# A hybrid encoder step on one core: where the moving operands begin, and 35 products behind the last one

## The reference

```
h   = x @ w_in                    # 2048 -> 5124: RG-LRU x and gate, band q,k,v, FoX q,k,v, forget logits
y_A = RG-LRU(conv4(x branch)) * gelu(gate)
y_B = chunk-band attention        # 4 heads of 128
y_C = forgetting attention        # 4 heads of 128
x   = LN1(alpha * x + concat(rms(y_A), rms(y_B), rms(y_C)) @ w_out)
x   = LN2(alpha * x + square(relu(x @ w_up)) @ w_down)      # 2048 -> 8192 -> 2048
```

## Time and profile before

| | |
|---|---|
| median of 3 runs | 2268.21 us |
| profiled execution, from its first to its last instruction | 2264.6 us |
| what lies around it, median less span | 3.6 us |
| PE busy | 2246.3 us (99%), 16556 instructions |
| PE weight loads busy | 2195.6 us |
| DVE busy | 1719.4 us (76%) |
| ACT busy | 1046.0 us (46%) |
| TensorE clock granted | 0.999 of full |
| transfers | 459.60 MB, mean 203 GB/s |

### The profile page before, as it was taken

One profiled execution on the slowest core, in us unless ns is written; L12 is line 12 of the kernel. 1 busy time (PEld: TensorE's weight loads), 2 busy tenths in 40 slices (PEclk: granted clock), 3 DMA queues, 4 the chain that ended last, 5 costly groups with the idle time before them and its releaser, 6 DMA issues.

```text
span 2264.6 us, 38827 instructions
## 1 busy us (share of the span) xinstructions
PE 2246.3 (99%) x16556; PEld 2195.6 (97%) x16556; DVE 1719.4 (76%) x1314; ACT 1046.0 (46%) x1050; POOL 254.7 (11%) x273
## 2 busy tenths in 40 slices
PE   9999999999999999999999999999999999999998
PEld 8999999998889999999999999999999999999997
DVE  5667899885567766767777778778778878878887
ACT  4434566554444456654444444454345235335243
POOL 2010212210111032000000000001112102112101
PEclk9999999999999999999999999999999999999999
DMA  9775766776444487674555455679689789769875
GB/s 289 251 227 163 211 170 188 211 218 221 147 141 131 151 265 227 196 252 150 185 166 183 147 174 169 203 245 241 174 237 244 189 221 260 192 164 292 236 211 178
DMA packets 423343, 459.60 MB, mean 203 GB/s; under 512 B 16376, under 2 KB 398368, under 8 KB 422696
## 3 DMA queue, kind: packets, MB, share of 16 engines
q1 hardware_dynamic: 342608, 358.22, 50.3%
q0 software_dynamic: 36080, 52.64, 13.2%
q10 hardware_dynamic: 44520, 46.80, 6.1%
HBM read 371.12 MB, written 88.05 MB: 203 GB/s over the span
## 4 chain that ended last, share of the span: by engine, by line
PE 86%; DVE 5%; DMA 4%; ACT 2%; issue 1%; SPq 0%; ACTq 0%; DVEq 0%
PE psum L3097 55%; PE psum L2823 17%; PE psum L3066 4%; PE psum L513 4%; DMA raw<-in_w_down 2%; PE psum L3041 1%; DVE w_lo L2153 1%; PE psum L2903 1%; PE psum L2986 1%; PE psum L3002 1%; DVE x_e_lo L2293 1%; DVE w_lo L1706 1%; PE psum L2815 1%; PE psum L2982 0%; DMA kc<-in_cache_band_k 0%
## 5 line engine op out<-in xcount | busy, mean ns | idle before, releaser
L3097 PE MATMUL psum<-x_e_hi,w_hi 128*128 128x288 f32 x1600 | 474.6, 297 | 1.0 <-DVE w_lo L2153 0.8
L3097 PE MATMUL psum<-x_e_hi,w_lo 128*128 128x288 f32 x1600 | 474.2, 296 | 0.0
L3097 PE MATMUL psum<-x_e_lo,w_hi 128*128 128x288 f32 x1600 | 466.8, 292 | 0.0
L3097 PE MATMUL psum<-x_b_hi,w_hi 128*128 128x288 f32 x1536 | 455.4, 296 | 2.6 <-DVE w_lo L2153 1.2
L3097 PE MATMUL psum<-x_b_hi,w_lo 128*128 128x288 f32 x1536 | 455.3, 296 | 0.0
L3097 PE MATMUL psum<-x_b_lo,w_hi 128*128 128x288 f32 x1536 | 447.9, 292 | 0.0
L3097 PEld LDWEIGHTS psum<-x_e_lo,w_hi 128*128 128x128 f32 x1600 | 304.8, 190 | 0.0
L3097 PEld LDWEIGHTS psum<-x_e_hi,w_hi 128*128 128x128 f32 x1600 | 300.7, 188 | 2.7 <-DVE w_lo L2153 2.3
L3097 PEld LDWEIGHTS psum<-x_e_hi,w_lo 128*128 128x128 f32 x1600 | 300.0, 187 | 0.0
L3097 PEld LDWEIGHTS psum<-x_b_lo,w_hi 128*128 128x128 f32 x1536 | 292.8, 191 | 0.1
L3097 PEld LDWEIGHTS psum<-x_b_hi,w_hi 128*128 128x128 f32 x1536 | 288.6, 188 | 3.9 <-issue 2.0
(11 more groups left out here) (434 smaller groups left out, 4859.7 us busy)
## 6 DMA issues: line engine op xcount, KB each, us to landing
raw<-in_w_down SPq DMA_DIRECT2D x61, 1024.0 KB, 7.1
raw<-in_w_up SPq DMA_DIRECT2D x54, 1024.0 KB, 6.5
raw<-in_w_in SPq DMA_DIRECT2D x34, 1024.0 KB, 7.2
a_even<-in_w_down SPq DMA_DIRECT2D x30, 1024.0 KB, 7.2
raw<-in_w_out SPq DMA_DIRECT2D x24, 1024.0 KB, 5.5
a_even<-in_w_up SPq DMA_DIRECT2D x24, 1024.0 KB, 6.8
h_scratch<-c_tile ACTq DMA_DIRECT2D x48, 288.0 KB, 2.3
down_scratch<-c_tile POOLq DMA_DIRECT2D x45, 288.0 KB, 5.0
```

The source lines that it names most:

```text
L3097: mm = pe.matmul(PS[:, bank, 0:HALF], w, x[:, k, :], start=(k + n == 0), stop=(k == UK - 1 and n == 2))
```

## The change

There are two edits. The filler takes 104 bytes in place of 72. The tile behind it begins at 68864 = 538 x 128, and all tiles behind move up by 32 bytes: what began 96 past a multiple of 128 now begins on one. Operands that were at 224 or 96 past a multiple of 256 are now at 0 or 128 past one. Weights, `ident` and `ones` don't move.

Behind the last product PE has 35 more, in fp32r, after a wait for `rows_c` of 20: seven forms, five times each, with `x1_e1_hi` as moving and `w_hi` as stationary operand, into banks 0 to 3. Their results are not read.

```diff
@@ -130,7 +130,7 @@
-        sb("align_64_bytes", [128, 18])
+        sb("align_64_bytes", [128, 26])
@@ -3289,6 +3289,12 @@
+            pe.wait_ge(rows_c, 20)
+            spare_x, spare_w = (t[0][:, :, :].rearrange("p k c -> p (k c)") for t in (F5, WH))
+            for bank, (n, w_cols, x_at, w_at) in enumerate(((288, 96, 0, 0), (288, 64, 0, 0), (288, 128, 0, 16), (288, 128, 0, 8), (256, 128, 0, 0), (320, 128, 0, 0), (384, 128, 0, 0))):
+                for _ in range(5):
+                    pe.matmul(PS[0:w_cols, bank % 4, 0:n], spare_w[:, w_at:w_at + w_cols], spare_x[:, x_at:x_at + n], start=True, stop=True)
```

## The result

The changed kernel is slower. It takes 2274.86 us, the median of 8 runs (2272.8 to 2277.62), beside 2268.66 us for the kernel before (8 runs, 2266.6 to 2274.24). The ratio is 1.0025, with a 95% interval from 1.0015 to 1.0034. The prediction had said 2138 us. The profiled executions have spans of 2271.0 and 2264.6 us: 6.4 us more, about the 6.2 us between the medians.

What follows compares the result with a forecast made beforehand. PE's distance between product starts was taken as the bound. From 2264.6 us, 157 us saved less 27 lost to DVE gave 130 off, 2134.6, plus 3.6 for the median: 2138 us; range 2118 to 2290.

Steps and rivals of the forecast that it cites:

- The first candidate: PE: the weight load as cause of the lost 10 ns; set aside, as it allows a start every 127 ns or less.
- Ten are 133.3 ns, the number of L3066's last units to the tenth.: PE's moving operand: from 96 past, ten blocks of 128 bytes are fetched whole, 13.3 ns each, instead of nine.
- without the tenth block I take 120 ns and the 2.5 ns of the plain products, 122.5: Filler's effect on PE: fp32r products of 288 columns fall from 132.5 to 122.5 ns; 157 us over all lines before losses.
- N: Rival, PE: the loss comes with any fp32r product at one clock a column, so moving operands does nothing; 2268 us, chance 0.18.
- P: Rival, PE: only part is gained, by fetches of 64 bytes (2175 us) or a partial address effect (2221 us); chance 0.15.
- S: Rival, PE: slower, as fetches from the same half of 256 bytes wait; 135.8 ns a product, 2320 us; chance 0.25, mild form included.
- mild form: Milder slower rival, PE: all products cost the dearer half's 133.3 ns; 13 us more, 2281 us; more than half of 0.25.
- a distance that stays over 130 ns: Stated sign on PE that the prediction is wrong: the distance between product starts does not fall below 130 ns.
- The 27 us for DVE at its limit: DVE, late next once PE is faster: takes back 27 us of the gain, 10 at least and 45 at most.
- from 2118 to 2170: Whole kernel: range of the likeliest case, with 10 to 45 us lost and 122.5 to 124.5 ns a product; chance 0.42.
- the 32 bytes do nothing to DVE, ACT and the transfers: DVE, ACT and transfers: their operands move by the same 32 bytes, put at no cost.
- The 35 products were put at nothing: Kernel's end on PE: they take 4.5 us, covered by the last transfer with 2 us to spare, so cost nothing.

Runs made afterwards that it cites:

- e3: The changed kernel with stretches of 24 equal products in place of the 35, moving operand's start varied; 288 columns in fp32r cost 131.7 or 133.3 ns, bf16 122.6.
- e8: The changed kernel with stretches of 24 products in place of the 35, stationary start and width varied too; 32 stationary columns cost 130.4 ns where 128 cost 133.3.
- e9: The changed kernel with fp32r/bf16 pairs, 32-row products and 320 to 480 columns in place of the 35; pairs took 271.1 ns (288 columns) and 460 (512).
- e6: The kernel before with weights moved by 96 bytes and moving operands left in place; 2276.23 us, ratio 1.004, 133.1 ns a product of L3097.
- e7: The change without its 35 products, weights moved by the same 32 bytes as the moving operands; 2266.14 us, ratio 0.999 to before, 132.5 ns in L3097.
- e2: The kernel before, filler of 72 bytes kept, with only the 35 products added; 2269.27 us, ratio 1.0006.

## Why the prediction was wrong, by its steps

*What bounds the kernel, and what a product costs.* Right. PE set the time before and sets it now, 132.5 ns were the distance, 122.5 is what 288 columns cost without the loss (bf16: 122.6), and 10 ns a product were lost. The first candidate was rightly put aside in part: a load of 32 columns gives back 3 of the 10 ns. For the rest the prediction leaned on one product with no load behind it and on L2843, where the distance stays at 133.1 while the stationary operand begins elsewhere with every block. But 133.1 is a mean over 32 products, and a mean over many starts can't show what one of them does. L2843 takes 8.85 us before and 8.84 after: the loss that depends on the address is in it both times.

*"Ten are 133.3 ns, the number of L3066's last units to the tenth."* This step failed, and with it the term of the sum that rests on it, "without the tenth block I take 120 ns and the 2.5 ns of the plain products, 122.5": 10.0 ns less a product were forecast, and 0.6 ns more were measured in L3097. It took 133.3 = 10 x 13.3 for a sign of ten fetched blocks. One number met one formula with a free count in it, and nothing in the trace varied the count. Nine blocks cost 133.4 (e3, L3297) and ten cost 131.7 (L3311). The other support, that plain float32 loses nothing from 96 past a multiple, was true and fitted every account in which four bytes a clock are too many, N's as well: "a new stream that must be filled at double rate". e8 and e9 have that loss from every start, and growing with the columns.

*The second row was there.* The trace showed one line with the same tiles at two prices, 131.8 and 133.3, by a shift of 128 bytes. That was the only effect of an address in the trace, 1.5 ns, and it was noted ("if only 1.5 ns of it"), but the forecast put 10 ns on the address. The change swaps these two cases. By this row alone the time moves by little, in either direction. So it was in L3066, where the two halves changed places.

*The rivals.* N had 2268 us, and P's cause, a smaller unit, is refuted with the forecast's. S in its mild form had 0.8 ns a product, 13 us and 2281; measured are 0.61 ns on L3097, 6.2 us between the medians and 2274.9. The sign was that of S, and in L3097 its words fit, too: all products cost what the dearer ones cost. Its mechanism doesn't fit: by it all products would do so everywhere, but L3066's first half rose from 131.8 to 133.3 while its second fell from 133.3 to 131.7. And what counts is the moving start relative to the stationary one (e6, e7), which none of the four cases had. "All moving operands have the same remainder" was half of the address. The range from 2118 to 2290 us took the measured time in by the shares of N and S, which the forecast spoke against; that is no merit of its sum. By its own sign, a distance that stays over 130 ns, the prediction is wrong.

The Trainium skill (TensorE: Matmul & The Clock Gate, section "Wait — 56ns, not 53.3ns?") has N / 2.4 + 2.5 ns warm, and in its section "Back-to-back issue gap" N / 1.2 cold. bf16 (122.6 by 122.5) and the lower clock (347 by 346.7) agree; fp32r at the higher clock doesn't, by 8 to 16 ns, with the moved start as without. Its lines of 16 bytes (SBUF — State Buffer, section "Door 1: The DMA port swizzle") would have treated before and after alike. Their N was nearer than the forecast, but 1.0025 isn't 1 either, and starts 32 bytes apart, whole lines all, cost 131.7 or 133.3.

*The terms behind the sum.* The 27 us for DVE at its limit were never called on, as PE didn't become faster; whether they were right stays untested. Its case "from 2118 to 2170" was too narrow for its own terms: 124.5 ns a product and 45 us lost are 2187. That the 32 bytes do nothing to DVE, ACT and the transfers held: 2292 ns for `w_lo` of `sigma`, 1917 for `w_hi`, beside the earlier trace rows, and `raw` and `a_even` land after 6.9 and 7.1 us, beside the earlier trace rows. The groups by form after:

```profile
L2153 DVE TENSOR_TENSOR w_lo<-sigma,w_hi 128x2048 fp32r<-128x2048 f32 x56 | 128.4, 2292 | 68.6 <-ACT w_hi L1499 67.2 <-ACT w_hi L1492 1.4
L1499 ACT ACTIVATE w_hi<-sigma 128x2048 fp32r<-128x2048 f32 x55 | 105.4, 1917 | 233.0 <-PE psum L3097 126.1 <-DVE sigma L2139 106.9
```

The 35 products were put at nothing because the last transfer covers them. That held with 1.4 us to spare (2 foreseen), and e2 confirms it. They take 5.4 us in place of 4.5, or of the 5.0 that the price "at 133 ns" had; 0.5 us of it lies between the first start and the second. Their groups of five gave 118, 147 and 177 ns for 256, 320 and 384 columns in the records, and are too few to tell 1.5 ns; e3 and e8 repeat them 24 times.

*What 6.4 us are made of.* PE is busy in L3097 for 1438.4 us, against 1430.9, 7.6 more. In L2823 it is busy for 459.8 us against 458.0, 1.8 more, and in L513 for 111.0 against 112.9, 1.9 less; L3066 and L2843 are the same to 0.02 us. Line L3097 after (stretch, us, PE busy, PEld):

```profile
0.00:2271.00 2271.00, 1438.41 (x10752) 1432.95 (x10752) 1.00 0.69 202
```

That makes 7.4 us of products, and 0.9 us come back by a wait that is now shorter. Waits of PE by line and releaser, before and after (us in total, times, longest):

```profile
PE psum L3097 <- DVE w_lo L2153: 2.0, 4, 1.2
```
```profile
PE psum L3097 <- DVE w_lo L2153: 1.1, 3, 0.7
```

## What to carry to other kernels

Where a whole kernel waits for one product form, vary that form by itself (24 in a row behind the last one cost 3 us) before a mechanism is read out of the kernel's mean: a formula that meets one number to the tenth has not been tested. Of two operands read side by side, look at both addresses; here their difference modulo 256 bytes counted and neither alone, and from block to block the order of the differences as well. And let a forecast claim from an address no more than the rows show that an address does, which was 1.5 ns of 10.

## What the runs showed of the hardware

- Products of 288 columns in fp32r behind each other, with 128 stationary columns, cost 131.5 to 131.9 ns or 133.0 to 133.5, by moving start less stationary start modulo 256 bytes (0 and 96 cheap; 32, 128, 160, 192 and 224 dear; 64 at 131.7 in one stretch, 132.4 and 132.3 in two others). bf16 costs 122.6. No stretch of 288 columns in fp32r had a mean under 130 ns, not even with a load of 32 columns.
- fp32r loses at 2.4 GHz, 8 to 11 ns a product from 256 to 384 columns and 13 to 16 from 416 to 512 (32 stationary columns), and nothing at 1.2 GHz (347 ns for 416 columns). At 512 columns and 128 stationary ones it has 228 or 232 ns where bf16 has 216.
- Two alternating differences don't always cost the mean of their single prices: 0 and 128 cost 133.1 for 132.5.
- An fp32r and a bf16 product in turns cost 271 ns a pair at 288 columns and 460 at 512, 15 and 12 more than the sum of the two alone.
